# Mixer layers of a six-sublayer transformer: 18 convolution taps move to GpSimd, and scores, gelu, pool parts, transposes and out chunks take another order

## The reference

```python
h = rms_norm_2(x, norm_mix_pre[l])
z = h @ w_in[l]
za, zq, zkv, zg, zc, zd = jnp.split(z, offsets, axis=-1)
y_conv = conformer_conv(za, ...)      # a * sigmoid(gate); causal depthwise convolution, 31 taps, 256 channels; layer norm; silu
y_nsa = nsa_attention(zq, zkv, ...)   # 4 heads; compressed, selected and window branches, gated
y_sgu = spatial_gating(zc, ...)       # gelu, layer norm, 128x128 causal mix, product
y_pool = multiscale_pool(zd, ...)     # windows 2, 4, 8, 16, a small mix, a scale
y = jnp.concatenate([y_conv, y_nsa, y_sgu, y_pool], axis=-1) @ w_out[l]
x = x + rms_norm_2(y, norm_mix_post[l])
```

## Time and profile before

| | us |
|---|---|
| median of 3 runs | 1981.53 |
| the profiled execution, its own time | 1979.86 |
| its span | 1978.2 |
| TensorE busy | 1854.0 |
| VectorE busy | 1429.3 |
| ScalarE busy | 939.7 |
| GpSimd busy | 130.1 |

### The profile page before, as it was taken

One profiled execution on the slowest core, in us unless ns is written; L12 is line 12 of the kernel. 1 busy time (PEld: TensorE's weight loads), 2 busy tenths in 40 slices (PEclk: granted clock), 3 DMA queues, 4 the chain that ended last, 5 costly groups with the idle time before them and its releaser, 6 DMA issues.

```text
span 1978.2 us, 32149 instructions
## 1 busy us (share of the span) xinstructions
PE 1854.0 (94%) x11902; PEld 1654.1 (84%) x11902; DVE 1429.3 (72%) x2221; ACT 939.7 (48%) x1357; POOL 130.1 (7%) x168
## 2 busy tenths in 40 slices
PE   2999999899999999999999999999789998789998
PEld 2999877799989997888878799978579987659997
DVE  6778898677787778677665555556768865867984
ACT  2444465454435443455454444444564445654443
POOL 1001111000110000000000000000011200001110
PEclk8999999989998999899999999999899998999999
DMA  9777765357787777354540255554145554224453
GB/s 365 268 272 280 279 232 204 118 188 279 271 302 256 275 269 272 120 186 173 188 149 1 86 209 190 179 207 150 51 173 188 176 191 148 107 82 153 177 185 126
DMA packets 61539, 382.11 MB, mean 193 GB/s; under 512 B 6896, under 2 KB 6896, under 8 KB 24448
## 3 DMA queue, kind: packets, MB, share of 16 engines
q1 hardware_dynamic: 41040, 300.96, 42.2%
q0 software_dynamic: 19984, 77.93, 11.1%
q10 hardware_dynamic: 432, 2.08, 0.3%
HBM read 379.89 MB, written 1.05 MB: 193 GB/s over the span
## 4 chain that ended last, share of the span: by engine, by line
PE 86%; DVE 8%; ACT 3%; issue 2%; DMA 1%; SPq 0%; DVEq 0%; ACTq 0%
PE ps L478 13%; PE ps L479 13%; PE ps L480 13%; PE ps L444 11%; PE ps L446 11%; PE ps L445 11%; PE ps L762 1%; DVE arena L1989 1%; PE ps L499 1%; PE ps L525 1%; PE ps L501 1%; PE ps L500 1%; DMA arena<-in_mod 1%; DVE ring_lo L1461 1%; PE ps L550 1%
## 5 line engine op out<-in xcount | busy, mean ns | idle before, releaser
L1461 DVE TENSOR_TENSOR ring_lo<-ring,w_hi 128x1024 fp32r<-128x1024 f32 x534 | 648.7, 1223 | 354.2 <-ACT w_hi L1055 350.2
L1055 ACT ACTIVATE w_hi<-ring 128x1024 fp32r<-128x1024 f32 x556 | 586.7, 1059 | 633.9 <-PE ps L480 325.4
L478 PE MATMUL ps<-h_lo,w_hi 128*128 128x256 f32 x2112 | 601.5, 285 | 10.4 <-issue 5.9
L479 PE MATMUL ps<-h_hi,w_hi 128*128 128x256 f32 x2112 | 600.7, 284 | 0.0
L480 PE MATMUL ps<-h_hi,ring_lo 128*128 128x256 f32 x2112 | 600.5, 284 | 0.0
L478 PEld LDWEIGHTS ps<-h_lo,w_hi 128*128 128x128 f32 x2112 | 407.5, 193 | 12.0 <-issue 7.2
L479 PEld LDWEIGHTS ps<-h_hi,w_hi 128*128 128x128 f32 x2112 | 407.5, 193 | 0.0
L480 PEld LDWEIGHTS ps<-h_hi,ring_lo 128*128 128x128 f32 x2112 | 407.4, 193 | 0.0
L444 PE MATMUL ps<-w_hi,h_lo 128*128 128x512 f32 x604 | 247.9, 410 | 21.4 <-DVE h_lo L2066 6.8
L446 PE MATMUL ps<-w_hi,h_hi 128*128 128x512 f32 x604 | 240.6, 398 | 0.0
L445 PE MATMUL ps<-ring_lo,h_hi 128*128 128x512 f32 x604 | 240.4, 398 | 0.0
(11 more groups left out here) (320 smaller groups left out, 1924.6 us busy)
## 6 DMA issues: line engine op xcount, KB each, us to landing
ring<-in_stream SPq DMA_DIRECT2D x278, 1024.0 KB, 4.8
arena<-in_mod POOLq DMA_DIRECT2D x128, 512.0 KB, 5.4
arena<-in_mod SPq DMA_DIRECT2D x3, 2048.0 KB, 17.2
gate<-in_wide POOLq DMA_DIRECT2D x3, 1536.0 KB, 10.1
arena<-in_nsaw POOLq DMA_DIRECT2D x2, 1072.0 KB, 8.9
arena<-in_mod SPq DMA_DIRECT2D x1, 1536.0 KB, 26.4
arena<-in_konst POOLq DMA_DIRECT2D x1, 1295.5 KB, 8.5
arena<-in_mixw POOLq DMA_DIRECT2D x2, 576.0 KB, 9.8
```

Of the source, the lines that this page charges most:

```text
L478: nc.tensor.matmul(dst, hi, x_lo, start=(r == 0 and i == 0 and b % 2 == 0), stop=False)
L479: nc.tensor.matmul(dst, hi, x_hi, start=False, stop=False)
L1055: nc.scalar.activation(w_hi[:, q % SPLITS, :], ring[:, half % SLOTS, (q % 2) * QUARTER:(q % 2 + 1) * QUARTER], ACT.Copy).then_inc(w_hi_rea ...
L1461: v.tensor_tensor(ring_lo[:, slot, cs], ring[:, slot, cs], w_hi[:, q % SPLITS, :], ALU.subtract).then_inc(w_lo_ready, 1)
```

## The change

GpSimd gets a function `convolution(l)`: it waits for `cv_ready`, multiplies taps 13 to 30 with their weights (128x512, the weight of each channel broadcast along time) and adds them up in `cfar`, in the memory of `xn`, with `cd` and `csq` in turns as the product's place. That is 18 multiplies and 17 adds; each add waits for its own engine's instructions before it. The last one signals `conv_far`. VectorE does taps 0 to 12 and then adds `cfar` to `cacc`. `convolution(0)` stands behind the `wide` load for FFN 4 and ahead of the next DMA issues, `convolution(1)` between the splits of the two FFNs. The orders of the three other engines' mixer programs change as the diff shows.

```diff
-TAPS = 31
+TAPS, TAPS_V = 31, 13
+        cfar = xn[:, 0, 0:512].rearrange("p (c t) -> p c t", c=2)
+            def convolution(l):
+                def wide_col(o):
+                    return cols[:, o:o + 2].unsqueeze(2).broadcast_to([P, 2, T])
+                pool.wait_ge(cv_ready, l + 1)
+                for k in range(TAPS_V, TAPS):
+                    if k >= TAPS_V + 2:
+                        tick.settle(1)
+                    tap = cfar if k == TAPS_V else (cd, csq)[k % 2]
+                    tick.mark(nc.gpsimd.tensor_tensor(tap, cv[:, :, k:k + T], wide_col(COLS["conv_w"] + (l * TAPS + k) * 2), ALU.mult))
+                    if k > TAPS_V:
+                        tick.settle()
+                        ins = nc.gpsimd.tensor_tensor(cfar, cfar, tap, ALU.add)
+                        if k < TAPS - 1:
+                            tick.mark(ins)
+                ins.then_inc(conv_far, 1)
...
             wide(6, 0, 3).then_inc(gate_in, 16)
+            convolution(0)
             pool.wait_ge(x_ready, 14)
             wide(9, 0, 1).then_inc(gate_in, 16)
             pool.dma_start(nsaw, a["nsaw"][1, :, :]).then_inc(mix_in, 16)
             pool.dma_start(mixw, a["mixw"][1, :, :]).then_inc(mix_in, 16)
             split(4)
+            convolution(1)
             split(5)
# TensorE
                 scores(0)
                 pooled()
                 part(3, 2, bA)
+                scores(1)
                 mixed()
-                scores(1)
                 part(3, 3, bA)
...
                 values(1)
+                turn_probs(2)
                 gating()
-                turn_probs(2)
                 values(2)
+                turn_gating()
                 turn_probs(3)
-                turn_gating()
                 pe.wait_ge(sgu_out, l + 1)
-                out_chunk(2)
-                values(3)
                 pe.wait_ge(conv_ready, l + 1)
...
                 mm.then_inc(mu_sum, 1)
+                values(3)
+                out_chunk(2)
                 out_chunk(3)
# ScalarE
                 exps(0)
+                split(q0 + 16, q0 + 17)
                 act.wait_ge(pool_sum, l + 1)
                 nc.scalar.activation(pT, ps[:, 7, :], ACT.Copy).then_inc(pool_copied, 1)
-                split(q0 + 16, q0 + 17)
                 exps(1)
                 weighed(0)
-                weighed(1)
-                split(q0 + 17, q0 + 18)
+                nc.scalar.activation(warm[:, :], eps_col, ACT.Gelu_apprx_tanh)
                 act.wait_ge(quarter_done, q0 + 16)
...
                 ins.then_inc(pool_hi, 1)
-                split(q0 + 18, q0 + 19)
+                split(q0 + 17, q0 + 18)
+                weighed(1)
                 act.wait_ge(zvar_ready, l + 1)
...
+                split(q0 + 18, q0 + 19)
                 exps(2)
                 weighed(2)
-                split(q0 + 19, q0 + 20)
                 exps(3)
                 weighed(3)
-                split(q0 + 20, q0 + 21)
+                split(q0 + 19, q0 + 20)
                 act.wait_ge(sgu_T, l + 1)
...
-                split(q0 + 21, q0 + 22)
+                split(q0 + 20, q0 + 22)
# VectorE
-                taps(5, 7)
+                taps(5, 8)
                 split(q0 + 14, q0 + 15)
-                taps(7, 10)
                 dve.wait_ge(d_copied, l + 1)
...
-                taps(10, 14)
                 dve.wait_ge(kv_sum, 3 * l + 3)
...
                 split(q0 + 15, q0 + 16)
-                taps(14, 16)
                 maxes(0)
                 maxes(1)
-                taps(16, 17)
+                taps(8, 9)
                 weigh(0)
                 split(q0 + 16, q0 + 17)
+                maxes(2)
+                maxes(3)
                 weigh(1)
-                taps(17, 19)
-                maxes(2)
-                split(q0 + 17, q0 + 18)
-                maxes(3)
-                taps(19, 21)
+                taps(9, 11)
```

More of the change, by code:

```diff
@@ L293, in build @@
         cact_ready = sem("cact_ready")
-        dve_tick, act_tick = sem("dve_tick"), sem("act_tick")
+        dve_tick, act_tick, pool_tick = sem("dve_tick"), sem("act_tick"), sem("pool_tick")
+        conv_far = sem("conv_far")
         x_ready, x_half = sem("x_ready"), sem("x_half")
@@ L382, in split @@
                         step(PEEL + r, it)
+            tick = Tick(pool, pool_tick)
+            def convolution(l):
[13 more added lines that the diff above has]
+                ins.then_inc(conv_far, 1)
             def mod_load(q, r):
@@ L2042, in mixer @@
                 split(q0 + 15, q0 + 16)
-                taps(14, 16)
                 maxes(0)
                 maxes(1)
-                taps(16, 17)
+                taps(8, 9)
                 weigh(0)
                 split(q0 + 16, q0 + 17)
+                maxes(2)
+                maxes(3)
                 weigh(1)
-                taps(17, 19)
-                maxes(2)
-                split(q0 + 17, q0 + 18)
-                maxes(3)
-                taps(19, 21)
+                taps(9, 11)
+                dve.wait_ge(pool_hi, l + 1)
+                for c in range(2):
+                    ins = v.scalar_tensor_tensor(out=h_lo[:, 6 + c, :], in0=ps[:, 7, c * T:(c + 1) * T], scalar=col("pool_s", 2 * l + c),
+                                                 in1=h_hi[:, 6 + c, :], op0=ALU.mult, op1=ALU.subtract)
+                ins.then_inc(pool_out, 1)
+                take_probs(0)
                 dve.wait_ge(b_gelu, l + 1)
@@ L2062, in mixer @@
                 ins.then_inc(zvar_ready, 1)
[L2063 to L2071, removed]
+                split(q0 + 17, q0 + 18)
+                taps(11, TAPS_V)
                 dve.wait_ge(zstd_ready, l + 1)
@@ L2081, in mixer @@
                 v.tensor_tensor(vn, vn, ln[1], ALU.add).then_inc(vn_ready, 1)
+                split(q0 + 18, q0 + 19)
                 weigh(2)
                 take_probs(1)
-                split(q0 + 19, q0 + 20)
-                weigh(3)
-                taps(25, 28)
                 dve.wait_ge(sgu_sum, l + 1)
@@ L2092, in mixer @@
                 ins.then_inc(sgu_ready, 1)
+                weigh(3)
                 take_probs(2)
-                split(q0 + 20, q0 + 21)
-                taps(28, TAPS)
+                split(q0 + 19, q0 + 20)
                 flat = lambda w, c: w[:, c:c + 2, :].rearrange("p c t -> p (c t)")
@@ L2098, in mixer @@
                 v.tensor_tensor(flat(h_lo, 4), ps[:, 6, :], flat(h_hi, 4), ALU.subtract).then_inc(sgu_out, 1)
+                dve.wait_ge(conv_far, l + 1)
+                v.tensor_tensor(cacc, cacc, cfar, ALU.add).then_inc(conv_ready, 1)
                 take_probs(3)
-                split(q0 + 21, q0 + 22)
+                split(q0 + 20, q0 + 22)
                 dve.wait_ge(mu_sum, l + 1)
```

## The result

The changed kernel takes 2010.78 us (median; 2008.69 to 2013.07), the kernel before 1982.14: ratio 1.0152, 95% interval 1.0131 to 1.0174. It is 1.5% slower, 29 us; I had forecast 1965 as the likeliest, and the measured time lies just outside my range for 8 in 10, 1959 to 2010.

What follows compares the result with a forecast made beforehand. TensorE, busy 94% of the span, was taken as the bound, so only its gaps and low-clock time could be won. Net 8.1 us a mixer, 16.2 for both, gave 1965 us; own range 1959 to 1976, 8 in 10: 1959 to 2010.

Steps and rivals of the forecast that it cites:

- Rival A: VectorE's two-SBUF-input instructions wait for GpSimd's in progress: 32 us blocked before kcT, +22 to +34 us in all; chance 0.28.
- Rival B: VectorE mostly goes first and GpSimd waits, ending 4 to 12 us late: 1973 to 1990 us; chance 0.22.
- Parts 1 to 6: In each mixer, fewer VectorE taps and the new order: 11.2 us gained, 3.1 given back, net 8.1.
- Gelu's wait: In the mixer, TensorE waits 1.5 us for gelu instead of 4.2, since gelu ends earlier.
- the pool's: TensorE's wait for the pool's low part before chunk 0 shrinks from 3.7 us to 0.3.
- values: Behind chunk 0, TensorE waits 1.4 us around take_probs(1) and 2.9 around take_probs(2), part of the time given back.
- part 5: With shorter TensorE gaps, out chunk 0 runs wholly at the high clock: 2.7 us more a mixer, bounds 0 and 2.7.
- a sign of being wrong: The forecast is wrong if waits behind chunk 0 exceed the 11.2 us gained, or the low clock returns there.
- Part 7: GpSimd's 35 instructions at 1.25 us take 47 us, done at 1398, before VectorE asks at 1417, delaying nothing.
- My cover of 13: Before kcT, VectorE's idle time (1.6 + 6.9 us) and six fewer taps (4.8) absorb 13 us of blocking.
- Rival C: GpSimd is simply slow, 2.4 us an instruction, ending 21 us late: +12 us a mixer, 2006 us; chance 0.05.

Runs made afterwards that it cites:

- e4: The changed kernel with each GpSimd product and sum cut in two of 128x256, same arithmetic: 1988.25 us, ratio 1.0037.
- e3: The changed kernel with GpSimd's 35 products and sums replaced by 51 memsets, taps 13 to 30 left out: 1970.97 us, ratio 0.9966.
- e7: The changed kernel with GpSimd's convolution also waiting for kv_ready, so starting only when kcT is copied: 1998.07 us, ratio 1.0095.
- e1: The changed kernel without GpSimd's convolution, taps 13 to 30 left out, VectorE keeping 13 taps and the add: 1967.86 us, ratio 0.9924.
- e5: The changed kernel's new order without GpSimd's convolution, all 31 taps on VectorE, 18 put where it stood idle: 1967.10 us, ratio 0.9946.

## Why the prediction was wrong

**What failed.** Not a term of the sum, but the assumption under it: that VectorE's instructions keep their lengths beside GpSimd. In its place the trace shows a tap every 1.31 us instead of 0.40, a split of 2.1 to 2.3 instead of 1.2, and kcT 21.6 us later than without GpSimd. I had written that no row bears on it, gave it 0.43, and gave the rule of the Trainium skill (SBUF — State Buffer, section "Who interferes with whom") 0.50 in Rivals A and B. By that rule the traces agree: exclusion for whole instructions (e4), reading against two-input instructions (e3), operands from PSUM unhurt (0.42 and 0.94 in e7). As I had put it, for two inputs alone, it left out the gates, the copy and tap 0. In the absence of a row the sum should have been made with the rule and not without.

**Parts 1 to 6** stand in the total; the clock is less sure than I made it. e1 is that forecast: 1967.9 for 1965. In mixer 0, counted from the first split shown, its last out matmul starts at 1442.86 - 1352.66 = 90.2 us, before it was 1450.24 - 1351.69 = 98.6: 8.4, for my 8.1. Gelu's wait was 1.8 for 1.5, the pool's 0.5 for 0.3, chunk 0 at the high clock, values 3.7 for 1.4 + 2.9, the wait before the mean 0.4. But mixer 1 of the same execution, the slowest of e1's four, gained only 1.0 (1766.17 - 1669.44 = 96.7 for 97.7). TensorE waits no longer there than in mixer 0, but the granted clock (the third value from the end in these stretches) was low in chunk 0 and again behind it:

```profile
1715.05:1719.46 4.41, 4.41 (x12) 3.24 (x12) 4.38 (x11) 4.36 (x10) 0.00 (x0) 0.64 0.19 80
1732.80:1745.50 12.70, 12.30 (x36) 7.26 (x36) 6.57 (x8) 4.78 (x9) 0.00 (x0) 0.50 0.00 0
```

The high clock of chunk 0 in part 5 is thus not assured by shorter gaps, and the low clock behind chunk 0, which I had named as a sign of being wrong, does come. e5, whose profiled execution was its fastest, gained 8.8 and 7.8 in the two mixers by the same count.

**Part 7** was right that GpSimd is in time: 1349.06 to 1400.21, 51 us for my 47. A multiply alone takes 1.04; I took 1.25 for each. What was wrong was to look only at its end.

**Rival A** was the mechanism, and its price near. I had 27 x 1.2 = 32 us of blocking before kcT. VectorE's rows between 1349.1 and 1400.3 us; before, the mean lengths were 477, 1220 and 164 ns:

```profile
L2012 DVE SCALAR_TENSOR_TENSOR arena<-arena,cols 128x256 f32<-128x256 f32 x14 | 18.4, 1376 | 0.0
L1484 DVE TENSOR_TENSOR ring_lo<-ring,w_hi 128x1024 fp32r<-128x1024 f32 x7 | 13.0, 1864 | 2.4 <-ACT w_hi L1078 2.4
L2056 DVE TENSOR_SCALAR g<-gt 128x4 f32<-128x4 f32 x5 | 3.5, 757 | 0.0
```

14 taps at +0.90 make 12.6 us, the five splits between tap 0 and kcT 3.8, rotations and blk 7.4: 24 for the 27 that I had counted, 0.9 each and not 1.2. But gates, a copy and tap 0, with one SBUF input, were hit too, which I had not counted: 5.4 more, 29 in all. My cover of 13 was right: 29 - 13 = 16, and kcT came at 47.0 for 31.0 before, counted from the split. TensorE then stood 10.4 + 5.5 = 16 us for my 19, and the low clock took most of the rest, which I had left out. While TensorE waits for kcT and just after, the granted clock of the changed kernel falls to 0.69 and 0.53, most of it at the 1.2 GHz level; from 1430 to 1440 it is 0.67 once more:

```profile
1384.00:1397.30 13.30, 2.87 (x14) 2.04 (x14) 13.30 (x16) 0.60 (x1) 12.91 (x11) 0.69 0.24 79
1397.30:1403.00 5.70, 5.70 (x40) 4.75 (x40) 3.83 (x18) 0.62 (x3) 2.83 (x2) 0.53 0.01 3
```

The last out matmul starts at 1464.26 - 1349.95 = 114.3 us, 15.7 behind before and 24.1 behind e1. Mixer 1 is 13.3 behind before (111.0 for 97.7): 29 for both, the 29 measured; Rival A said 22 to 34.

**Rivals B and C** fall. VectorE does not go first: they alternate one for one. GpSimd's instructions are not slow: 1.04 us for an unhindered multiply, where Rival C needed 2.4.

## What to carry to other kernels

Arithmetic given to GpSimd with inputs in SBUF can be paid for by VectorE: here nearly every VectorE instruction with two SBUF inputs beside it waited for a GpSimd instruction to end, 0.9 us on average, so count VectorE's critical instructions in that stretch, not GpSimd's microseconds. If it must be, short GpSimd instructions cost less (e4), and so does a stretch with fewer of such VectorE instructions ahead of something that TensorE waits for (e7); VectorE's work on PSUM kept its length there. Neither got the loss back whole. Before moving work off an engine that is not the bound, look for its idle time: here the 18 taps fitted into it at no cost that the runs could tell.

## What I had not expected of the hardware

Where both engines have work ready the turns are one for one, and GpSimd suffers far less. Its last instructions in e7, beside which VectorE stood idle for 6.4 us, show the undisturbed pace:

```profile
1420.45 1.04 POOL L398 TENSOR_TENSOR arena<-arena,cols 128x512 f32<-128x512 f32 x1
1421.57 1.27 POOL L401 TENSOR_TENSOR xn<-xn,arena 128x512 f32<-128x512 f32 x1
1422.79 1.04 POOL L398 TENSOR_TENSOR arena<-arena,cols 128x512 f32<-128x512 f32 x1
```

That is 2.34 us for a product and a sum, so by my estimate 41 us for all 35; beside VectorE's taps it took 51, a quarter more, while those taps take 3.3 times as long.

A scalar operation of 4 elements takes 0.76 us on average instead of 0.16 beside GpSimd, and tap 0 is held up even by memsets (1.09 us an instruction in e3, 0.41 before), while two-input taps are not. Not every instruction with one SBUF input is: the batch statistics, beside GpSimd in e7, kept their length (0.73 for two, 0.75 before).
